# Attention scores of a transformer layer as seven block products instead of eight, with the norm's factor in the softmax

## The reference

```python
x = x + rmsnorm(mix, norm_mix_post[l])
xa = memory_cross_attention(rmsnorm(x, norm_x_pre[l]), rmsnorm(mem, norm_mem[l]), w_xq[l], w_xkv[l], w_xo[l])
x = x + rmsnorm(xa, norm_x_post[l])

def memory_cross_attention(xn, memn, w_xq, w_xkv, w_xo):      # 4 heads of 256
    q, k, v = ...
    s = jnp.einsum('bshd,bmhd->bhsm', q, k) * (X_HEAD_DIM ** -0.5)
    p = jax.nn.softmax(s, axis=-1)
    o = jnp.einsum('bhsm,bmhd->bshd', p, v).reshape(B, S, D_MODEL)
    return o @ w_xo
```

## Time and profile before

| | us |
|---|---|
| median of 3 runs | 1251.17 (1250.87 to 1251.33) |
| profiled execution: its span | 1249.9 |
| what the median has above this span | 1.3 |
| PE busy | 1239.3 (99%) |
| DVE busy | 792.1 (63%) |
| ACT busy | 566.9 (45%) |
| POOL busy | 240.3 (19%) |

### The profile page before, as it was taken

The page is one execution under the profiler, slowest core; times in us unless marked ns, Lnnn a source line. Parts: engine busy times, 40 slices in busy tenths (PEclk is TensorE's granted clock), DMA queues, the critical chain, the costliest instruction groups (busy, mean ns, idle before and its releaser), DMA issues.

```text
span 1249.9 us, 17399 instructions
## 1 busy us (share of the span) xinstructions
PE 1239.3 (99%) x6456; PEld 1037.9 (83%) x6456; DVE 792.1 (63%) x1144; ACT 566.9 (45%) x1021; POOL 240.3 (19%) x362
## 2 busy tenths in 40 slices
PE   9999999999999999999999999999999999999998
PEld 8998987878888888888878888888888888888886
DVE  6862666467864653546886666767866756565646
ACT  6575546564433532435554333333333334545432
POOL 1323122040110200021200000013554545000003
PEclk9999999999999999999999999999999999999999
DMA  9989677574410211121223545556654557897723
GB/s 383 389 271 378 171 224 206 163 185 152 169 67 36 85 51 51 52 84 68 73 103 119 204 180 188 209 189 224 235 173 152 176 201 248 288 339 232 239 86 135
DMA packets 76340, 224.33 MB, mean 179 GB/s; under 512 B 9040, under 2 KB 9184, under 8 KB 76256
## 3 DMA queue, kind: packets, MB, share of 16 engines
q1 hardware_dynamic: 59040, 163.95, 37.6%
q0 software_dynamic: 15776, 54.03, 13.3%
q10 hardware_dynamic: 1440, 5.24, 1.0%
HBM read 171.80 MB, written 68.16 MB: 192 GB/s over the span
## 4 chain that ended last, share of the span: by engine, by line
PE 91%; DMA 4%; issue 2%; DVE 2%; ACT 1%; POOL 1%; DVEq 0%; ACTq 0%; POOLq 0%
PE ps L2065 30%; PE ps L2066 29%; PE ps L2067 29%; DMA block_su_t<-in_w_in 2%; PE ps L2096 1%; DMA raw<-in_w_xkv 1%; DMA raw<-in_w_in 1%; PE ps L2218 1%; ACT ps L1062 0%; DVE w_lo L644 0%; DMA mem_first<-in_mem_t 0%; POOL rstd L915 0%; PE ps L2125 0%; PE ps L2166 0%; ACT w_hi L635 0%
## 5 line engine op out<-in xcount | busy, mean ns | idle before, releaser
L2065 PE MATMUL ps<-w_hi,act_hi 128*128 128x512 f32 (+1 forms) x448 | 171.0, 382 | 0.0
L2067 PE MATMUL ps<-w_hi,act_lo 128*128 128x512 f32 (+1 forms) x448 | 167.9, 375 | 0.0
L2066 PE MATMUL ps<-w_lo,act_hi 128*128 128x512 f32 (+1 forms) x448 | 167.8, 375 | 0.0
L2066 PE MATMUL ps<-act_lo,w_hi 128*128 128x512 f32 x384 | 149.4, 389 | 0.0
L1801 DVE TENSOR_TENSOR w_lo<-wraw,w_hi 128x512 fp32r<-128x512 f32 x126 | 95.9, 765 | 74.2 <-ACT w_hi L1281 74.1
L2065 PE MATMUL ps<-sums_hi,w_hi 128*128 128x512 f32 x352 | 137.2, 390 | 0.8 <-issue 0.8
L2067 PE MATMUL ps<-sums_hi,w_lo 128*128 128x512 f32 x352 | 137.0, 389 | 0.0
L1281 ACT ACTIVATE w_hi<-wraw 128x512 fp32r<-128x512 f32 x126 | 78.6, 628 | 90.5 <-PE ps L2067 71.0
L2065 PE MATMUL ps<-act_hi,w_hi 128*128 128x512 f32 x296 | 115.4, 390 | 0.1
L2067 PE MATMUL ps<-act_hi,w_lo 128*128 128x512 f32 x296 | 115.2, 389 | 0.0
L1807 DVE TENSOR_TENSOR w_lo<-wraw,w_hi 128x1024 fp32r<-128x1024 f32 x53 | 69.1, 1305 | 57.5 <-ACT w_hi L1292 57.2
(11 more groups left out here) (313 smaller groups left out, 2622.6 us busy)
## 6 DMA issues: line engine op xcount, KB each, us to landing
wraw<-in_w_ffn_gu SPq DMA_DIRECT2D x42, 512.0 KB, 4.3
hidden_a<-ffn POOLq DMA_DIRECT2D x44, 256.0 KB, 3.4
hidden_s<-ffn POOLq DMA_DIRECT2D x44, 256.0 KB, 2.3
wraw<-hidden_s SPq DMA_DIRECT2D x35, 256.0 KB, 3.4
wraw<-down_sums SPq DMA_DIRECT2D x31, 256.0 KB, 4.5
wraw<-in_w_ffn_down SPq DMA_DIRECT2D x27, 256.0 KB, 4.4
b_raw<-in_w_in SPq DMA_DIRECT2D x12, 512.0 KB, 5.1
block_vg_t<-in_w_in POOLq DMA_DIRECT2D x6, 1024.0 KB, 9.0
```

Source lines behind the costliest of these rows:

```text
L2065: nc.tensor.matmul(out_, lh, rh, start=first, stop=False, skip_group_check=onto)
L2066: nc.tensor.matmul(out_, lh, rl, start=False, stop=False, skip_group_check=onto)
L2067: return nc.tensor.matmul(out_, ll, rh, start=False, stop=last, skip_group_check=onto)
```

## The change

The stage `s` (16 steps of 24 matmuls) is replaced by a stage `at` of seven block products p1, p2, p6, p5, p3, p7, p4, 4 steps of 12 matmuls each. AT is the number of its first step, O0 = AT+28 that of the first step of `o`.

- The tokens are transposed from `resid` itself, without the norm's factor. That factor (`x1_rstd`) goes into the softmax, as scale of the exponential (`x1_scale`, `x1_neg`). The gain goes into the score weights when they are made, earlier in the kernel (line 1593 becomes a `scalar_tensor_tensor`), with a changed sign for the blocks that are subtracted.
- Operand sums: s1, s2, s3 by DVE (three additions for each of token tiles 4 to 7), s4 by POOL (`fourth_sum`). They are split by `a_split` (ACT and DVE, a quarter of an operand each, 128 x 4 x 128). Sums t1 to t4 of the score weights' blocks are made by POOL's DMAs. Blocks q = 28 to 41 (two halves for each product) are split by `block_split` into buffers c_hi, c_lo.
- The products: p1 and p6 are copied out of PSUM by ACT, p5 too; p2, p5, p3 and p7 are added by DVE. `at_evac` and `at_add` run in iteration n for step n-1. The scores stand in SBUF then (`half`, `tok4`), those of p4 in PSUM.
- The softmax of tile m (m from 0 to 15, 128 x 512 each): `maximum` on DVE and `exponent` on ACT in iteration `MAX_AT`, `denominator` on DVE one iteration later, and the division on POOL (`normalize`).
- The order of the iteration's parts on ACT: `at_evac`, `block_split`, `a_split`, `exponent`, copies of transposes. On DVE: `at_add`, `denominator`, `block_split`, `a_split`, `maximum`, subtractions for transposes.

```diff
+            STEPS += [("at", j, i) for j in range(7) for i in range(4)]
...
+    for q in range(2 * NB, 3 * NB):
+        BLOCK_AT[block_end(q) - 6 + q % 2] = q
+    BLOCK_AT[AT + 1], BLOCK_AT[AT + 2] = BLOCK_AT.pop(AT + 2), BLOCK_AT.pop(AT + 3)
...
+    A_SPLIT_AT = {AT + 1: [("s2", 0), ("s2", 1)], AT + 4: [("s2", 2)], AT + 5: [("s2", 3)]}
+    for i in range(4):
+        A_SPLIT_AT[AT + 8 + i] = [("s1", i)]
+        A_SPLIT_AT[AT + 12 + i] = [("s4", i), ("s3", i)]
...
+    MAX_AT = dict(zip([AT + n for n in (9, 10, 11, 12, 17, 18, 19, 20, 21, 22, 23, 24, 25, 26, 27, 28)], range(16)))
+    NORM_AT = {n + 1: m for n, m in MAX_AT.items()}
...
-        TR_AT[SNO["s", 1, t | 1] + LAG].append(("probs", t))
+        TR_AT[AT + (21, 21, 23, 23, 29, 29, 31, 31)[t]].append(("probs", t))
...
+            def normalize(m):
+                pool.wait_ge(den_ready, m + 1)
+                v = scores(m)
+                for h in range(2):
+                    ins = pool.tensor_scalar(v[:, h * NM:(h + 1) * NM], v[:, h * NM:(h + 1) * NM],
+                                             den[:, m % 2, h:h + 1], None, ALU.mult)
+                    if h == 0:
+                        ins.then_inc(pool_own, 1)
+                        own[0] += 1
+                ins.then_inc(probs_ready, 1)
...
+                    if t < 4:
+                        act.wait_ge(o_done, TT)
+                        act.wait_ge(ln_ready, TT)
+                        act.wait_ge(resid_ready, 4)
+                        nc.scalar.activation(x1_raw(t).rearrange("p k (b n) -> p k b n", b=2), halves,
+                                             ACT.Copy).then_inc(x_copied, 1)
+                        nc.scalar.activation(act_hi[:, :, cols].rearrange("p k (b n) -> p k b n", b=2), halves,
+                                             ACT.Copy).then_inc(tr_hi, 2)
+                    else:
+                        nc.scalar.activation(a_raw["s1"][:, :, low].rearrange("p k (b n) -> p k b n", b=2),
+                                             halves[:, 0:4], ACT.Copy).then_inc(x_copied, 1)
+                        nc.scalar.activation(act_hi[:, 4:8, cols].rearrange("p k (b n) -> p k b n", b=2),
+                                             halves[:, 4:8], ACT.Copy).then_inc(tr_hi, 2)
+                    return
...
+                elif kind == "at":
+                    at_evac(n, BLOCKS[b], t)
...
+            def at_evac(n, name, i):
+                if name not in ("p1", "p6", "p5"):
+                    return
+                act.wait_ge(mm_done, n + 1)
+                if name == "p1":
+                    act.wait_ge(resid_ready, 4 + i + 1)
+                    nc.scalar.activation(half[:, 4 + i, :], ps[:, x_of(i), :], ACT.Copy).then_inc(at_copied, 1)
+                elif name == "p6":
+                    act.wait_ge(s4_summed, 2)
+                    act.wait_ge(a_summed, 6)
+                    nc.scalar.activation(tok4[:, i, :], ps[:, x_of(i), :], ACT.Copy).then_inc(at_copied, 1)
+                else:
+                    nc.scalar.activation(q5[:, i, :], rolling(i), ACT.Copy).then_inc(at_copied, 1)
...
+            def exponent(m):
+                name, i = score_of(m)
+                t = score_token(m)
+                src = ps[:, x_of(i), :] if name == "c21" else scores(m)
+                factor = x1_scale if name in ("c11", "c12") else x1_neg
+                act.wait_ge(top_ready, m + 1)
+                if m >= 2:
+                    act.wait_ge(probs_ready, m - 1)
+                if name == "c21":
+                    act.wait_ge(s4_summed, 4)
+                for h in range(2):
+                    cs = slice(h * NM, (h + 1) * NM)
+                    ins = nc.scalar.activation(scores(m)[:, cs], src[:, cs], ACT.Exp, bias=top[:, m % 2, h:h + 1],
+                                               scale=factor[:, t:t + 1], accum_out=den[:, m % 2, h:h + 1])
+                    if h == 0:
+                        link(ins)
+                ins.then_inc(exp_ready, 1)
...
-                    nc.vector.tensor_tensor(stage_of(m), bank(n), mem_rows, ALU.mult).then_inc(free_dve, 1)
+                    g = (pre["x"] if (t < 4) == (b == 0) else x_neg)[:, t:t + 1]
+                    nc.vector.scalar_tensor_tensor(out=stage_of(m), in0=bank(n), scalar=g, in1=mem_rows,
+                                                   op0=ALU.mult, op1=ALU.mult).then_inc(free_dve, 1)
...
+                    nc.vector.tensor_tensor(s3, x, halves[:, 0:4], ALU.add).then_inc(a_summed, 1)
+                    nc.vector.tensor_tensor(s1, s1, halves[:, 4:8], ALU.add).then_inc(a_summed, 1)
+                    dve.wait_ge(a_summed, 3 * i + 1)
+                    nc.vector.tensor_tensor(s2, s3, halves[:, 4:8], ALU.add).then_inc(a_summed, 1)
+                    hi, lo = (w[:, 4:8, cols].rearrange("p k (b n) -> p k b n", b=2) for w in (act_hi, act_lo))
+                    nc.vector.tensor_tensor(lo, halves[:, 4:8], hi.bitcast(F32), ALU.subtract).then_inc(tr_lo, 2)
...
-                    def probs():
-                        dve.wait_ge(free_act, free_count(n, "act"))
-                        link(nc.vector.reciprocal(den[:, t % 2, :], den[:, t % 2, :]))
-                        dst = half[:, t, :] if b == 0 else tok[:, t % 2, 0:CW]
-                        for h in range(2):
-                            v = dst[:, h * NM:(h + 1) * NM]
...
+            def at_add(n, name, i):
+                if name not in ("p2", "p5", "p3", "p7"):
+                    return
+                dve.wait_ge(mm_done, n + 1)
+                if name == "p2":
+                    v = half[:, 4 + i, :]
+                    dve.wait_ge(at_copied, i + 1)
+                    nc.vector.tensor_tensor(v, v, rolling(i), ALU.subtract).then_inc(at_added, 1)
+                elif name == "p5":
+                    v = tok4[:, i, :]
+                    dve.wait_ge(at_copied, 8 + i + 1)
+                    nc.vector.tensor_tensor(v, v, rolling(i), ALU.add).then_inc(at_added, 1)
+                elif name == "p3":
+                    v = tok4[:, i, :]
+                    dve.wait_ge(at_added, 4 + i + 1)
+                    nc.vector.tensor_tensor(v, v, rolling(i), ALU.add).then_inc(at_added, 1)
...
+            def maximum(m):
+                name, i = score_of(m)
+                t = score_token(m)
+                src = ps[:, x_of(i), :] if name == "c21" else scores(m)
+                if name == "c21":
+                    dve.wait_ge(mm_done, SNO["at", 6, i] + 1)
+                elif name == "c22":
+                    dve.wait_ge(at_added, 12 + i + 1)
+                else:
+                    dve.wait_ge(at_added, (8 if name == "c12" else 0) + i + 1)
+                if m >= 2:
+                    dve.wait_ge(exp_ready, m - 1)
+                op, factor = (ALU.max, x1_neg) if name in ("c11", "c12") else (ALU.min, x1_scale)
+                link(nc.vector.tensor_reduce(top[:, m % 2, :], src.rearrange("p (h m) -> p h m", h=2), AX.X, op))
+                nc.vector.tensor_scalar(top[:, m % 2, :], top[:, m % 2, :], factor[:, t:t + 1], None,
+                                        ALU.mult).then_inc(top_ready, 1)
+            def denominator(m):
+                dve.wait_ge(exp_ready, m + 1)
+                nc.vector.reciprocal(den[:, m % 2, :], den[:, m % 2, :]).then_inc(den_ready, 1)
...
+            def denominator(m):
+                dve.wait_ge(exp_ready, m + 1)
+                nc.vector.reciprocal(den[:, m % 2, :], den[:, m % 2, :]).then_inc(den_ready, 1)
...
+                if n in NORM_AT:
+                    denominator(NORM_AT[n])
...
+                for name, i in A_SPLIT_AT.get(n, ()):
+                    a_split(name, i)
+                if n == AT + 9:
+                    score_factors()
+                if n in MAX_AT:
+                    maximum(MAX_AT[n])
...
+                elif name == "p6":
+                    pe.wait_ge(at_copied, i + 1)
+                elif name == "p7":
+                    pe.wait_ge(at_copied, 4 + i + 1)
+                elif name == "p4":
+                    pe.wait_ge(at_added, 12 + i + 1)
+                    pe.wait_ge(tr_lo, 2 * (TRNO["xn2", 4 + i] + 1))
+                else:
+                    r = 4 * ("p2", "p5", "p3").index(name) + i
+                    if r < 2:
+                        pe.wait_ge(tr_lo, 2 * (TRNO["xn2", 6] + 1))
+                    else:
+                        pe.wait_ge(at_added, r - 1)
+                    if 6 <= r < 10:
+                        pe.wait_ge(at_copied, 8 + r - 5)
+                need = {"p6": "s2", "p5": "s1", "p3": "s4", "p7": "s3"}.get(name)
+                if need:
+                    pe.wait_ge(operand_lo, KT + A_NO[need, i] + 1)
+                ts = slice(i * P, (i + 1) * P)
+                us = slice(CW + i * P, CW + (i + 1) * P)
+                for k in range(4):
+                    q = 2 * NB + 2 * j + k // 2
+                    if i == 0 and k % 2 == 0:
```

(18 more changed lines are left out.)

366 lines of the change are left out of this document (242 added, 124 removed).

## The result

The changed kernel takes 1265.24 us (median of 4 runs, 1262.43 to 1266.56) where the kernel before takes 1251.25 in the runs beside it. The ratio is 1.0108 (95% interval 1.0094 to 1.0122): 1.1% slower, some 14 us. The prediction said 1258.8, with 1264.5 as its upper end. The direction was right and the size was not: the change costs 14 us where 7.6 were forecast.

A forecast was written before the change was run, and what follows sets the result against it. The prediction took PE's matmuls and gaps as the bound: 81.6 + 3.1 + 8.8 + 6.8 = 100.3 us against 92.6 for the stage, 7.7 longer; with small corrections 1258.8 us, range 1249 to 1264.5.

The forecast's parts named there:

- What is removed: In the score stage, 336 matmuls in place of 384, 48 fewer: 10.9 us.
- First place: AT+2 to AT+7: PE's transposes and next steps wait for DVE's longer queue of sums and splits, 3.1 us.
- Second place: AT+9 to AT+14: PE waits in AT+12 (3.9 us) and before AT+14 for ACT's and DVE's tied queues, 8.8 us.
- The turn of 5.7: One iteration's round through ACT and DVE between AT+9 and AT+13, nothing overlapping: 5.7 us against 2.72 for PE's step.
- Third place: AT+17 to AT+24: the same tie with c12 and c22, 5.4 us of it in AT+24; 6.8 us in all.
- the rival on the clock: PE's clock falls in the long waits; three spells at 1.2 GHz, 2 us each, give 1264.8 us; chance 0.08.
- What I cost at nothing: POOL's division, block sums and loads by DMA, and the table load taken as hidden; the gain as 0 to 1 us.
- The table load: Before the first exponential: 1.28 us, done 0.7 us before the first maximum, hidden; by the skill page 0.6 us more.
- The other side: Rival: the turn is shorter and the stage gains, needing under 4.55 us for over 0.2%; chance 0.15.
- Its own signs: 48 fewer matmuls; PE waits in AT+12, before AT+14, in AT+24; turns of 5.7 us; clock 1.00.

The follow-up runs named there:

- the experiment without the sum: The changed kernel with POOL writing zeros in place of the sum s4: 1261.15 us, ratio 1.0071.
- the experiment with the maximum first: The changed kernel with DVE's maximum ahead of the splits of block halves and quarters, the reciprocal behind them: 1251.87 us, ratio 0.9998.
- the filled waits: The changed kernel with 42 matmuls whose result nobody reads put in three waits of PE (AT+4, AT+12, before AT+14): 1261.39 us, ratio 1.0082.

## Why the prediction was right in its direction and wrong in its size

- **What is removed.** 48 matmuls, 10.9 us at 0.2266: right.
- **First place (3.1 us predicted).** AT+8 begins at 455.8, which is 30.8 after the end of `wo`'s last matmul, where 27.5 was predicted. The waits before the transposes were 1.1 and not 2.1, the order of the queues was right. Two things were missing: POOL's additions held the rest of q30 up by 1.8 us and that of q31 by 0.7 (the experiment without the sum), and the clock fell behind the wait of 2.55 us, which cost 1.7. Without the sum AT+8 begins at 26.7, near the prediction.
- **Second place (8.8 us predicted).** AT+9 to AT+14 took 22.1 us where 22.4 was predicted (458.55 to 480.63). The turn of 5.7 is measured at 5.70 and 5.66, and the experiment with the maximum first shows that it was the tie of ACT's and DVE's order. POOL had no part in it: DVE's rest of a block half takes 1.31 us within the turn, near the 1.22 of its price. The exponential of 0.60 is right.
- **Third place (6.8 us predicted).** From AT+14 to `o` 51.1 us in place of 47.6. The steps behind AT+14 ran at 1.2 GHz (14 matmuls, 3.0 us), and POOL's division took 1.3 us for 128x256, the upper end of what the earlier trace rows had bounded, and 2.6 for a tile, so that the transposes of tile 3 waited 1.8 and not 0.3 us for it, with 1.7 us of slow matmuls behind. The wait in AT+24, the longest of the prediction at 5.4 us, was 1.7, since PE came there late itself. So this place was wrong in its terms, and they made up for each other in part.
- **The first step that failed** is the rival on the clock: "the granted clock is 1.00 to 1249 and has a mean of 0.64 in the next microsecond; so a wait of 5.4 us is near what brought it down there, and one of 3.9 is not". Slow matmuls followed waits of 2.55, 3.58, 2.85 and 1.81 us, and in the kernel before one of 3.04. The last microseconds of the run say how late the records show a fall there and not how short a wait is enough. I gave it 0.08 and a price of 2 us for each wait. The price was about right (1.3 to 3 us each, 3.9 in all by the filled waits), though no row of before showed its spell of 4 us. Only the chance was far too low, and it should have been a term of the sum for each of the waits that the sum itself forecast.
- The Trainium skill, "TensorE: Matmul & The Clock Gate", section "HAM oscillation", was cited in the prediction as speaking for this rival, and the traces agree in most places: of the 17 waits of 2 us or more in this stage, over all profiled executions, 13 had slow matmuls behind them, and 4 (2.56, 2.82, 3.00 and 3.59 us) had none.
- **The second step that failed**, as large as the first, is a term put at nothing: POOL's hold on DVE. Under "What I cost at nothing" the prediction checked POOL's division for being late, and neither there nor in the first place what POOL's sum s4 does to its neighbour. It is worth 2 us of waits (2.55 against 0.50 in AT+4), and 4.1 in time with the clock behind them.
- **The table load.** In the kernel with the maximum first the exponential's maximum is ready early, and ACT shows nothing behind the load:

```profile
459.73 1.28 ACT L1345 ACT_TABLE_LOAD   x1
461.03 0.60 ACT L1345 ACTIVATE half<-half,top,x_scale 128x256 f32<-128x256 f32 x1
```

  The load lasts its 1.28 us, as in the earlier trace rows. The further 1.38 us of the page "ScalarE: Activation LUTs" of the Trainium skill, section "What ACT_TABLE_LOAD costs", are not there; the measurement decides.
- **The other side** ("the turn is shorter") had the point from which it decides at 4.55 us. With the maximum first the turn is 3.3 us and the loss is gone. The claim that a microsecond in the turn is worth 9 us is too high: 2.4 us bought 13.4, 5.6 each, and some of that is the clock.
- **Its own signs.** The turns of 5.7 us and the first two of the three places of PE's waits came true. Three signs went the other way: AT+8 began at 30.8 and not near 27.5, PE waited for POOL, and the clock didn't stay at 1.00.

What stays open: why the changed kernel's runs differ by 4 us. The mean clock of the runs goes with it (0.998 in the run of 1262.43, 0.992 in that of 1266.56), which fits waits that sometimes bring the clock down and sometimes not, as the traces have it (2.55 us with slow matmuls behind and 2.56 without, at the same place), but no experiment took it apart.

## What to carry to other kernels

Where two engines with queues of their own pass work to each other within an iteration, add up one round along both queues before the count of instructions: an exponential that waits for a maximum which stands behind splits that wait for the exponential's engine costs the sum of both, and putting the maximum first gave 13 us back. When a forecast finds waits of PE of two microseconds or more, give each one a price for the slow clock behind it as well, 1.3 to 3 us here in three cases of four. Work that is moved to POOL should be put where DVE reads PSUM or is idle: POOL's additions stopped a DVE instruction that reads only SBUF until they had ended, 1.8 us here.
